# Expert gate and up products in a diffusion trunk: token slots as the stationary operand, weights split on chip and streamed

## The reference, cut to what matters

```python
D_MODEL, SEQ, N_EXPERTS, TOP_K, D_FF_EXPERT = 1024, 256, 8, 2, 1408

def swiglu(h, wg, wu, wd):
    return (jax.nn.silu(h @ wg) * (h @ wu)) @ wd

def moe_swiglu(h, w_r, b_r, wg, wu, wd):
    ...                       # softmax router, two experts of eight per token
    y = jnp.zeros_like(h)
    for e in range(N_EXPERTS):
        y = y + combine[..., e:e + 1] * swiglu(h, wg[e], wu[e], wd[e])
    return y
```

## Time and profile before

| | us |
|---|---|
| median of three runs (lowest, highest) | 1632.26 (1626.22, 1633.0) |
| the profiled execution, its own time | 1623.51 |
| span in its trace | 1621.7 |
| one trip of the experts' loop | 62.1 |
| from the end of the first gather to the last down product (8 trips) | 497.9 |

### The profile page before, as it was taken

The page is one execution under the profiler, slowest core; times in us unless marked ns, Lnnn a source line. Parts: engine busy times, 40 slices in busy tenths (PEclk is TensorE's granted clock), DMA queues, the critical chain, the costliest instruction groups (busy, mean ns, idle before and its releaser), DMA issues.

```text
span 1621.7 us, 22792 instructions
## 1 busy us (share of the span) xinstructions
PE 1491.6 (92%) x9198; PEld 1245.7 (77%) x9198; DVE 801.8 (49%) x1340; ACT 423.5 (26%) x779; POOL 343.1 (21%) x272
## 2 busy tenths in 40 slices
PE   5799999788979999999979995769999999999996
PEld 2587877454468888888859983669999999999995
DVE  2843424776374344344477745634444444444353
ACT  2311133363120110010032143522323323323321
POOL 0109999900010000000013998000000000000000
PEclk9899999899989999999989997979999999999999
DMA  8235542362212222222313310039776776877800
GB/s 363 86 149 217 232 156 104 140 222 106 103 53 102 81 104 104 94 86 95 109 52 137 117 53 0 1 158 424 293 286 259 290 282 263 308 266 258 314 16 26
DMA packets 30017, 263.92 MB, mean 163 GB/s; under 512 B 3328, under 2 KB 3328, under 8 KB 4224
## 3 DMA queue, kind: packets, MB, share of 16 engines
q1 hardware_dynamic: 29952, 263.01, 42.9%
HBM read 261.95 MB, written 1.05 MB: 162 GB/s over the span
## 4 chain that ended last, share of the span: by engine, by line
PE 79%; DVE 8%; POOL 8%; ACT 2%; issue 2%; DMA 1%; SPq 0%; DVEq 0%; ACTq 0%
PE ps L427 34%; PE ps L795 19%; PE ps L780 7%; POOL sb_arena L1641 4%; PE ps L673 4%; POOL sb_arena L1644 3%; PE ps L440 2%; PE ps L754 2%; PE ps L764 2%; PE ps L457 1%; DVE sb_rows_n L1371 1%; PE ps L559 1%; PE ps L546 1%; DMA sb_arena<-mod 1%; PE ps L606 1%
## 5 line engine op out<-in xcount | busy, mean ns | idle before, releaser
L795 PEld LDWEIGHTS ps<-sb_H,sb_arena 128*128 128x128 f32 x2816 | 326.0, 192 | 6.6 <-issue 1.2
L795 PE MATMUL ps<-sb_H,sb_arena 128*128 128x128 f32 x2816 | 327.3, 275 | 1.0 <-DVE sb_H L1503 1.0
L427 PE MATMUL ps<-sb_h_hi,sb_w_hi 128*128 128x512 f32 (+1 forms) x640 | 241.6, 378 | 9.8 <-DVE sb_h_lo L1189 9.8
L427 PE MATMUL ps<-sb_h_lo,sb_w_hi 128*128 128x512 f32 (+1 forms) x640 | 240.7, 376 | 0.0
L427 PE MATMUL ps<-sb_h_hi,sb_w_lo 128*128 128x512 f32 (+1 forms) x640 | 240.6, 376 | 0.0
L1188 DVE CAST sb_w_hi<-sb_arena 128x2048 fp32r<-128x2048 f32 (+1 forms) x58 | 73.0, 1258 | 215.4 <-PE ps L427 139.8
L1641 POOL TENSOR_SCALAR sb_arena<-sb_arena,sb_small 128x512 f32<-128x512 f32 (+1 forms) x120 | 175.9, 1466 | 11.8
L1520 DVE TENSOR_TENSOR sb_ew_lo<-sb_arena,sb_ew_hi 128x1024 fp32r<-128x1024 f32 x88 | 107.7, 1224 | 85.3 <-ACT sb_ew_hi L1072 84.3
L427 PEld LDWEIGHTS ps<-sb_h_hi,sb_w_hi 128*128 128x128 f32 x640 | 121.8, 190 | 32.4 <-DVE sb_h_lo L1189 10.6
L1644 POOL TENSOR_TENSOR sb_arena<-sb_arena 128x512 f32<-128x512 f32 (+1 forms) x120 | 139.1, 1159 | 10.0
L427 PEld LDWEIGHTS ps<-sb_h_hi,sb_w_lo 128*128 128x128 f32 x640 | 121.7, 190 | 21.8
(11 more groups left out here) (273 smaller groups left out, 2282.5 us busy)
## 6 DMA issues: line engine op xcount, KB each, us to landing
sb_arena<-experts SPq DMA_DIRECT2D x88, 1536.0 KB, 8.0
sb_arena<-mod SPq DMA_DIRECT2D x48, 1024.0 KB, 5.0
sb_arena<-in SPq DMA_DIRECT2D x24, 1024.0 KB, 4.8
sb_arena<-gate SPq DMA_DIRECT2D x11, 1024.0 KB, 4.8
sb_arena<-up SPq DMA_DIRECT2D x11, 1024.0 KB, 4.7
sb_arena<-out SPq DMA_DIRECT2D x8, 1024.0 KB, 4.7
sb_arena<-down SPq DMA_DIRECT2D x8, 1024.0 KB, 4.8
sb_arena<-down SPq DMA_DIRECT2D x4, 768.0 KB, 4.1
```

The costliest lines, as they stand in the source:

```text
L427: ins = pe.matmul(o, left[a], right[b], start=(k == first and n == 0), stop=(k == final and n == len(PRODUCTS) - 1))
L795: ins = pe.matmul(ps[:, 2 + f % 2, a * P:(a + 1) * P], w[:, k, :], h_slot[:, k, :], start=(k == 0), stop=(k == KD - 1))
```

## The change

Only `moe()` and the layout of the expert weights change.

- **Gate and up.** The slots become the stationary operand, split into `hs_hi` (ACT, at the copy out of the gather) and `hs_lo` (DVE). The weights of gate and up become the moving operand, in halves of 1024 columns: ACT writes the leading part (`glead`, four buffers in space that is free by then), DVE the rest (`egu_lo`). The products are triple fp32r ones. The host lays the weights out so that two tiles of f make a pair: a matmul of 512 columns gives 256 gate and 256 up columns. The pair is complete when both its tiles have been streamed; the eleventh tile stands alone, with 256 columns.
- **Hidden values** now come out slot-major. DVE multiplies SiLU(gate) with up (`hidden_product`), TensorE turns the tile (`turn_hidden`), ACT and DVE split the turned values (`hidden_leading`, `hidden_rest`).
- **Order.** Down of tile f runs behind gate and up of tile f+3 (f+1 before). The scatter is cut in two halves, in tiles 3 and 5, and uses banks 4 and 5; the copies of the finished output are both ACT's (`take_output`), at tile 1 of the next trip. An empty SiLU stands at the head of the loop on ACT.

```diff
+                    def gate_up(f):
+                        p = f // 2
+                        o = ps[:, 2 + p % 2, 0:2 * pair_width(p)]
+                        if f % 2 == 0:
+                            pe.wait_ge(hid_done, i * PAIRS + (PAIRS + p - 1))
+                        for a in range(2):
+                            pe.wait_ge(gu_split, i * 2 * ET + (2 * f + a + 1))
+                            lead = glead[(2 * f + a) % 4]
+                            rest = egu_lo[f][:, a * HALF:(a + 1) * HALF].rearrange("p (a n) -> p a n", a=4)
+                            tiles = 2 if pair_width(p) == 2 * P else 4
+                            first = (f % 2) * KD // 2 if tiles == 2 else 0
+                            for t in range(tiles):
+                                k = first + a * tiles + t
+                                span = slice(t * 4 // tiles, (t + 1) * 4 // tiles)
+                                for n, (x, w) in enumerate(((hs_hi, lead), (hs_hi, rest), (hs_lo, lead))):
+                                    ins = pe.matmul(o, x[:, k, :], w[:, span, :], start=(k == 0 and n == 0),
+                                                    stop=(k == KD - 1 and n == 2))
+                            ins.then_inc(gu_used, 1)
+                    def turn_hidden(p):
+                        pe.wait_ge(hid_done, i * PAIRS + (PAIRS + p + 1))
+                        pe.wait_ge(glu_done, i * PAIRS + (PAIRS + p - 1))
+                        for j in range(pair_width(p) // P):
+                            ins = pe.transpose(ps[:, 6 + p % 2, j * P:(j + 1) * P], epair[:, p % 2, j * P:(j + 1) * P], ident)
+                        ins.then_inc(turned, 1)
...
                     for f in range(ET):
-                        pe.wait_ge(sem_exp[f], i * 16 + 16)
-                        if f == 0:
-                            pe.wait_ge(h_act, i + 1)
-                            pe.wait_ge(h_dve, i + 1)
-                        last = f - 2 + ET if f >= 2 else max(x for x in range(ET) if x % 2 == f)
-                        pe.wait_ge(glu_done, i * ET + (last + 1))
-                        for a in range(2):
-                            w = experts[:, f, a * KD * P:(a + 1) * KD * P].rearrange("p (k n) -> p k n", k=KD)
-                            for k in range(KD):
-                                ins = pe.matmul(ps[:, 2 + f % 2, a * P:(a + 1) * P], w[:, k, :], h_slot[:, k, :],
-                                                start=(k == 0), stop=(k == KD - 1))
-                        ins.then_inc(gu_full, 1)
-                        if f:
-                            down(f - 1)
-                        if f == 2:
-                            scatter(i)
+                        gate_up(f)
+                        if f >= 2 and f % 2 == 0:
+                            turn_hidden(f // 2 - 1)
+                        if f >= 3:
+                            down(f - 3)
+                        if f == 3:
+                            pe.wait_ge(y_act, i + 1)
+                            pe.wait_ge(from_slot_ready, i + 1)
+                            scatter(i, (0, 1))
                         if f == 5:
+                            scatter(i, (2, 3))
+                        if f == 6:
                             pe.wait_ge(shares_built, i + 1)
+                            pe.wait_ge(x_added, i * 4 + 5)
                             for b in range(2):
                                 ins = pe.transpose(ps[:, 4, b * P:(b + 1) * P], shares[:, b, :], ident)
                             ins.then_inc(shares_turned, 1)
+                    down(ET - 3)
                     pe.wait_ge(from_slot_ready, i + 2)
+                    pe.wait_ge(x_added, i * 4 + 6)
                     gather(i + 2)
+                    turn_hidden(PAIRS - 1)
+                    down(ET - 2)
                     down(ET - 1)
...
+                def take_output():
+                    for m in range(2):
+                        ins = f(y_slot[:, m * 512:(m + 1) * 512], ps[:, m, :], ACT.Copy)
+                    ins.then_inc(y_act, 1)
...
+                    def gate_up_leading(t):
+                        act.wait_ge(sem_exp[t], i * 16 + 16)
+                        for a in range(2):
+                            x = 2 * t + a
+                            act.wait_ge(gu_used, i * 2 * ET + (half_before(x) + 1))
+                            f(glead[x % 4], experts[:, t, a * HALF:(a + 1) * HALF].rearrange("p (a n) -> p a n", a=4), ACT.Copy)\
+                                .then_inc(gu_leading, 1)
+                    def leading(t):
+                        act.wait_ge(down_done, i * ET + (down_before(t) + 1))
+                        f(ew_hi[:, t % 2, :], experts[:, t, 2 * HALF:], ACT.Copy).then_inc(down_leading, 1)
+                    def silu(p):
+                        w = pair_width(p)
+                        act.wait_ge(gu_used, i * 2 * ET + (2 * ET + min(2 * (2 * p + 2), 2 * ET)))
+                        act.wait_ge(turned, i * PAIRS + (PAIRS + p - 1))
+                        f(epair[:, p % 2, 0:w], ps[:, 2 + p % 2, 0:w], ACT.Silu).then_inc(silu_done, 1)
+                    def hidden_leading(p):
+                        w = pair_width(p)
+                        act.wait_ge(turned, i * PAIRS + (PAIRS + p + 1))
+                        act.wait_ge(down_done, i * ET + (ET + 2 * p - 2 if p >= 2 else ET - 1 + p))
+                        f(e_hi2[:, p % 2, 0:w], ps[:, 6 + p % 2, 0:w], ACT.Copy).then_inc(e_leading, 1)
+                    f(spare, eps, ACT.Silu)
                     for t in range(ET):
-                        act.wait_ge(sem_exp[t], i * 16 + 16)
...
-                        f(ew_hi[:, t % 2, :], experts[:, t, 2 * KD * P:], ACT.Copy).then_inc(down_leading, 1)
-                        act.wait_ge(gu_full, i * ET + (t + 1))
...
-                        f(esilu[:, t % 4, :], ps[:, 2 + t % 2, 0:P], ACT.Silu).then_inc(silu_done, 1)
+                        gate_up_leading(t)
+                        if t == 1:
+                            act.wait_ge(down_done, i * ET + ET)
+                            act.wait_ge(scattered, i * 4 + 4)
+                            take_output()
+                        if t >= 3:
+                            leading(t - 3)
+                        if t >= 2 and t % 2 == 0:
+                            silu(t // 2 - 1)
+                        if t >= 3 and t % 2:
+                            hidden_leading((t - 3) // 2)
+                    hidden_leading(PAIRS - 2)
+                    leading(ET - 3)
+                    silu(PAIRS - 1)
+                    leading(ET - 2)
                     take_input(i + 2)
-                    act.wait_ge(down_done, i * ET + 2 * ET)
-                    f(y_slot[:, 0:512], ps[:, 0, :], ACT.Copy).then_inc(y_act, 1)
+                    hidden_leading(PAIRS - 1)
+                    leading(ET - 1)
...
                 def take_input(count):
-                    dve.wait_ge(gathered, count)
-                    v.tensor_copy(h_slot[:, 4:8, :], ps[:, 5, :].rearrange("p (k n) -> p k n", k=4)).then_inc(h_dve, 1)
+                    for b in range(2):
+                        dve.wait_ge(h_act, count * 2 + (b - 1))
+                        ins = v.tensor_tensor(hs_lo[:, 4 * b:4 * b + 4, :], ps[:, 4 + b, :].rearrange("p (k n) -> p k n", k=4),
+                                              hs_hi[:, 4 * b:4 * b + 4, :].bitcast(F32), ALU.subtract)
+                    ins.then_inc(h_dve, 1)
...
+                    def gate_up_rest(t):
+                        for a in range(2):
+                            x = 2 * t + a
+                            dve.wait_ge(gu_leading, i * 2 * ET + (x + 1))
+                            v.tensor_tensor(egu_lo[t][:, a * HALF:(a + 1) * HALF].rearrange("p (a n) -> p a n", a=4),
+                                            experts[:, t, a * HALF:(a + 1) * HALF].rearrange("p (a n) -> p a n", a=4),
+                                            glead[x % 4].bitcast(F32), ALU.subtract).then_inc(gu_split, 1)
+                    def rest(t):
+                        dve.wait_ge(down_leading, i * ET + (t + 1))
+                        v.tensor_tensor(ew_lo[t][:, :], experts[:, t, 2 * HALF:], ew_hi[:, t % 2, :].bitcast(F32),
+                                        ALU.subtract).then_inc(down_split, 1)
+                    def hidden_product(p):
+                        w = pair_width(p)
+                        dve.wait_ge(silu_done, i * PAIRS + (p + 1))
+                        v.tensor_tensor(epair[:, p % 2, 0:w], epair[:, p % 2, 0:w], ps[:, 2 + p % 2, w:2 * w], ALU.mult)\
+                            .then_inc(hid_done, 1)
+                    def hidden_rest(p):
+                        w = pair_width(p)
+                        dve.wait_ge(e_leading, i * PAIRS + (p + 1))
+                        v.tensor_tensor(e_lo2[:, p % 2, 0:w], ps[:, 6 + p % 2, 0:w], e_hi2[:, p % 2, 0:w].bitcast(F32),
```

(31 more changed lines are left out.)

102 lines of the change are left out of this document (66 added, 36 removed).

## The result

| | before | after |
|---|---|---|
| median of 20 runs, us | 1626.39 | 1632.66 |
| lowest, highest | 1623.27, 1633.0 | 1629.48, 1644.77 |
| the profiled execution's own time | 1623.51 | 1644.77 |

The ratio is 1.0041, with a 95% interval of 1.0028 to 1.0055: the changed kernel is some 6 us slower. I had forecast -2 us, 1630, no difference that can be told. The size is within the 0.5% that I called no change, but 20 runs a side resolve it, and it has the other sign. The profiled execution of after is the slowest of its 20, so it shows more of the trouble than a usual run, and not all of it belongs to the change. Its span is 21.3 us longer than that of before (1643.0 against 1621.7): 8.3 us lie ahead of the first gather (it starts at 1103.32, before at 1095.01), in code that is the same, 6.1 between the first gather and the last, 6.9 behind the last.

A forecast was written before the change was run, and what follows sets the result against it. TensorE was taken to bound the kernel. Eight trips of 61.2 us (53.8 work, 7.4 waits) plus entry, exit and clock gave 496 against 497.9 us, so -2: 1630 us, own range 1623 to 1641, wider range 1610 to 1654.

The forecast's parts named there:

- TensorE's work, 53.8 us a trip: Sum of TensorE's products, turns, gather and scatter in one trip after the change: 53.8 us, 8.3 less than before.
- VectorE below TensorE: In the steady tiles VectorE needs 7.6 us per two tiles against TensorE's 8.4; 48 against 53.8 a trip.
- The four waits and 61.2 us a trip: TensorE waits before tile 6 (2.4), down(8) (1.6), down(10) (2.4), next first tile (1.1): 7.4 us, trip 61.2.
- Entry, exit and transfers: Around the trips: entry +4.0 less 1.1, output copies at the end +0.5; transfers unchanged, ScalarE not waiting for DMA.
- The clock term, 2 us (0 to 5) for the first trip alone: First trip, behind 5 us of idleness, begins at 1.2 GHz: 2 us added, range 0 to 5.
- The argument behind that term: Behind 2.45 us idle the next 4 us ran at clock 1.00; no forecast wait exceeds 2.4 us.
- The rival: Clock falls in every trip: 5 us each at 1.2 GHz, TensorE loses 2.5; +20, 1652 us; chance 0.10.
- tile 6's waits: TensorE idle 2.4 us a trip ahead of tile 6, while VectorE adds the scatter's third quarter.

The follow-up runs named there:

- Experiment 8: The kernel of experiment 5 with one more unread VectorE product per expert tile: 46 columns, 1571.2 us; 512 columns, 1595.54 us (one run each).
- experiment 3: The changed kernel with VectorE's additions of the scatter's second half, and TensorE's share transposes, one tile later: 1614.89 us, ratio 0.9921.
- experiment 4: The changed kernel with only the trip's end reordered (last pair turned ahead of the gather, next trip's input taken later): 1613.98 us, ratio 0.9935.
- experiment 5: The changed kernel with the moves of experiment 3 and experiment 4, and the input's copies at the head of ScalarE's loop: 1570.9 us, ratio 0.9658.
- experiment 1: The changed kernel with unread TensorE products filling most of the waits at tile 6, down(8), down(10) and the trip's end: 1625.04 us, ratio 0.9993.
- experiment 6: The kernel of experiment 5 with the additions of quarters 2 and 3 back at tile 5, restoring the wait ahead of tile 6: 1596.42 us, ratio 0.9815.
- experiment 7: The kernel before the change with one TensorE wait per trip, behind tile 6's gate/up, for two GpSimd scalings: 1649.38 us, ratio 1.014.

## Why the prediction was right or wrong

- *TensorE's work, 53.8 us a trip*: right (53.9). The steps of 0.227 and 0.120 and the down products at fp32r speed came out as taken from the earlier trace rows. The Trainium skill, "TensorE: Matmul & The Clock Gate", section on the back-to-back issue gap, gives N / 2.4 + 2.5 ns as the gap of a single matmul, 0.216 us for 512 columns; the changed kernel, with other weights for each matmul, shows 0.227 where TensorE never waits.
- *VectorE below TensorE*: right, in size too: 1.216 us a subtraction, 7.6 against 8.4 us per pair of tiles. Experiment 8 measures its spare time: 4.2 us in 5.5 pairs of tiles, 0.76 per pair; the sum said 0.8.
- *The four waits and 61.2 us a trip*: right (61.26, each wait in its place with its releaser). Experiments 3 to 5 took them away or moved them, and each gave back its term in the undisturbed trips. (Two slips in the sums change nothing: the four terms add up to 7.5, not 7.4, and by its own terms the range is 1622 to 1640, not 1623 to 1641.)
- *Entry, exit and transfers*: right to some 2 us. From first gather to last, experiment 1 takes 492.5 us and before 498.4; behind the last gather 31.1 and 28.3, since the last trip's waits stand there; 1.6 more lie ahead of the experts, in code that is the same. The 31.1 were 32.8 but for the last sums of squares, which took 3.7 us at a clock of 1.00 there and 5.4 in before. ScalarE never waits for a transfer.
- *The clock term, 2 us (0 to 5) for the first trip alone*: **the step that failed.** It costs 7.6 us in the median by experiment 1, and more in the profiled execution: 12.0 over the seven trips (440.8 against 7 x 61.26) and 4.1 behind the last gather, where it takes 35.3 us and experiment 1 31.1 (1.7 of the 4.1 are the last sums again, as slow in before). -1.4 and +7.6 make the +6.3 measured.
- *The argument behind that term* was "behind 2.45 us the next 4 us ran at 1.00, and no place waits longer". It was one stretch of the earlier trace rows, read as a rule, and luck chose the stretch. In the same code other executions lose their clock there: experiment 4 behind that very wait of 2.45 us, the changed kernel for 20 us behind one of 2.15 just ahead of it, where before stayed at 1.00. The rows are of experiment 4 (two), the changed kernel and before:

```profile
365.31 1.07 PE L469 MATMUL ps<-sb_arena,sb_cond 128*32 128x256 f32 x16 [2.45 <-ACT sb_arena L1045]
367.10:370.50 3.40, 3.40 (x15) 0.51 0.87 301
356.00:376.00 20.00, 18.61 (x84) 0.50 0.43 158
356.00:376.00 20.00, 16.03 (x139) 1.00 0.59 211
```

Experiments 6 and 7 show the same inside one execution: a wait lets the clock fall in one trip and not in the next. The rival was there with the right mechanism (the clock falls in the trips), priced at 2.5 us a trip and given 0.10; it happened at some 1 us a trip in the median, and up to 2.5 in a trip of the profiled execution. It should have stood in the sum as a cost, not beside it as an accident: four waits a trip, each with some share of a 1.6 us loss.

The Trainium skill, same page, section "Why this matters for your kernels", advises against idle gaps of TensorE above some 3 us between bursts. The waits behind which the clock fell in the trips are all shorter, 2.05 to 2.2 us in the traces; the measurement decides.

What stays open: what settles, for a given wait, whether the clock falls. The strict alternation in experiment 6 suggests where in time the wait lies, but no run moved a wait by a known time to show it.

## What to carry over

A faster product moves the bound only as far as the feeders' order lets it: here 8.3 us of work a trip left TensorE and 7.4 came back as waits, all of them from the order in which two engines take their queues. Walk the queues at every place where an engine stands in a wait with someone else's work behind it, and move that work: the reorderings of experiment 5 made a kernel that is 3.4% faster than before, with the same arithmetic. And give every TensorE wait of 2 us a second price beside its own length: up to 1.6 us of clock behind it, which came behind two to six of seven such waits here. If it can't be removed, fill it.

## What the runs showed of the hardware

- Waits of 2.1 to 2.2 us in a stream otherwise dense let TensorE's granted clock fall to 1.2 GHz for a stretch that costs 1.6 us, and that can begin after 1.5 us of resumed work. It happened behind 3 of 7 such waits in experiment 6, 2 of 7 in experiment 7, and 6 of 7 of tile 6's waits in the profile of the changed kernel. With waits of 0.6 us or less (experiments 5 and 8) all trips had 1.00.
- Unread fp32 products of 128 columns keep the clock at 1.00, as long as they leave only short waits (0.5 us in experiment 1).
- The same code, in the same place, ran at 1.00 in one execution and at 0.50 for 20 us in another (356 to 376 us, before and the changed kernel). So the clock makes part of the spread between runs of one kernel, and one profile of a wait does not price it.
- VectorE's subtractions of 1024 columns took 1.217 us with TensorE at 99% and transfers at 316 GB/s, 1.224 in the kernel before: no contention to be seen.
